# The first loads, semaphore counts and two small activations of a two-layer trunk kernel are put in another order

## The reference

```python
for i in range(2):                                   # DEPTH layers, x is (1, 512, 1024) f32
    h = rms_norm(x, attn_norm_w[i])
    proj = h @ w_in[i]                               # 1024 x 7456
    dq, dk, dv, cq, ckv, krope, xq, gates = split(proj)
    # differential attention (8 heads), rope on the first 16 of 64 columns
    y_a = (rms_norm(diff_attention(rope(dq), rope(dk), dv, lam)) * (1 - lam_init)) @ w_o_diff[i]
    # latent attention: q and kv from low-rank cq, ckv, rope on 32 columns
    y_b = causal_attention(q_full, k_full, v_m) @ w_o_mla[i]
    # cross-attention into 256 memory tokens
    mk, mv = split(rms_norm(mem, mem_norm_w[i]) @ w_mem_kv[i])
    y_c = softmax_attention(xq, mk, mv) @ w_o_cross[i]
    g_a, g_b, g_c = split(sigmoid(gates))
    x = x + (g_a * y_a + g_b * y_b + g_c * y_c) @ w_out[i]
    f_gate, f_up = split(rms_norm(x, ffn_norm_w[i]) @ w_gate_up[i])
    x = x + (silu(f_gate) * f_up) @ w_down[i]
return rms_norm(x, final_norm_w)
```

## Time and profile before

| | |
|---|---|
| median of 3 runs | 1964.63 us |
| the profiled execution's own time | 1964.07 us |
| its span, first to last instruction | 1961.9 us |
| TensorE busy | 1947.8 us, 99% |
| TensorE weight loads busy | 1632.6 us, 83% |
| VectorE busy | 1037.2 us, 53% |
| ScalarE busy | 935.8 us, 48% |
| GpSimd busy | 1074.4 us, 55% |
| mean granted TensorE clock | 0.999 |

### The profile page before, as it was taken

How to read it: one execution, slowest core, us unless ns; L and a number is a source line. 1 busy time by engine, 2 the same in 40 slices (tenths; PEclk the granted TensorE clock), 3 DMA queues, 4 the chain that set the end, 5 groups by cost and what they waited for, 6 DMA issues and landing times.

```text
span 1961.9 us, 28882 instructions
## 1 busy us (share of the span) xinstructions
PE 1947.8 (99%) x9340; PEld 1632.6 (83%) x9340; DVE 1037.2 (53%) x1900; ACT 935.8 (48%) x1665; POOL 1074.4 (55%) x1422
## 2 busy tenths in 40 slices
PE   8999999999999999999999999999999999999998
PEld 7888888888888888888888888888888888888887
DVE  6445888887655333321144658888876443333111
ACT  6444666776544322233344456776674342222332
POOL 6654454445554555557765645344445555555674
PEclk9999999999999999999999999999999999999999
DMA  6443233224543333333344323223356333333232
GB/s 195 128 148 92 76 91 87 81 76 140 183 145 96 102 95 98 94 115 89 109 138 120 111 85 92 81 76 89 90 158 191 113 99 94 98 96 96 84 92 91
DMA packets 356001, 212.61 MB, mean 108 GB/s; under 512 B 14274, under 2 KB 339906, under 8 KB 355396
## 3 DMA queue, kind: packets, MB, share of 16 engines
q1 hardware_dynamic: 338288, 173.32, 30.7%
q10 hardware_dynamic: 17620, 38.07, 5.5%
HBM read 190.88 MB, written 20.45 MB: 108 GB/s over the span
## 4 chain that ended last, share of the span: by engine, by line
PE 98%; POOL 1%; DVE 0%; issue 0%; DMA 0%; ACT 0%; SPq 0%; POOLq 0%
PE proj L602 24%; PE proj L604 24%; PE proj L603 24%; PE score L602 2%; PE score L603 2%; PE score L604 2%; PE flip L656 2%; PE score L638 2%; PE score L816 1%; PE score L818 1%; PE score L642 1%; PE score L641 1%; PE att L583 1%; PE att L584 1%; PE att L582 1%; PE score L830 1%
## 5 line engine op out<-in xcount | busy, mean ns | idle before, releaser
L564 POOL TENSOR_TENSOR w_lo<-raw,w_hi 128x256 fp32r<-128x256 f32 x1376 | 1069.3, 809 | 866.1 <-ACT w_hi L1109 864.9
L602 PE MATMUL proj<-h_hi,w_hi 128*128 128x512 f32 x1584 | 626.3, 395 | 0.6 <-DVE h_lo L1977 0.3
L604 PE MATMUL proj<-h_hi,w_lo 128*128 128x512 f32 x1584 | 618.1, 390 | 0.0
L603 PE MATMUL proj<-h_lo,w_hi 128*128 128x512 f32 x1584 | 616.9, 389 | 0.0
L1109 ACT ACTIVATE w_hi<-raw 128x1024 fp32r<-128x1024 f32 x344 | 362.5, 1055 | 195.4 <-PE proj L604 55.2
L604 PEld LDWEIGHTS proj<-h_hi,w_lo 128*128 128x128 f32 x1584 | 297.3, 188 | 63.3
L602 PEld LDWEIGHTS proj<-h_hi,w_hi 128*128 128x128 f32 x1584 | 297.6, 188 | 60.6 <-issue 0.9
L603 PEld LDWEIGHTS proj<-h_lo,w_hi 128*128 128x128 f32 x1584 | 297.7, 188 | 58.9 <-issue 0.2
L602 PE MATMUL proj<-hid_hi,w_hi 128*128 128x512 f32 x330 | 129.0, 391 | 0.0
L604 PE MATMUL proj<-hid_hi,w_lo 128*128 128x512 f32 x330 | 128.5, 389 | 0.0
L603 PE MATMUL proj<-hid_lo,w_hi 128*128 128x512 f32 x330 | 128.4, 389 | 0.0
(11 more groups left out here) (420 smaller groups left out, 3147.2 us busy)
## 6 DMA issues: line engine op xcount, KB each, us to landing
raw<-in_w_in SPq DMA_DIRECT2D x224, 256.0 KB, 3.1
raw<-in_w_gate_up SPq DMA_DIRECT2D x176, 256.0 KB, 3.0
raw<-in_w_down SPq DMA_DIRECT2D x96, 192.0 KB, 2.5
gate_in<-gate_scratch ACTq DMA_DIRECT2D x48, 256.0 KB, 4.1
gate_scratch<-gate_out ACTq DMA_DIRECT2D x46, 256.0 KB, 2.0
raw<-in_w_mem_kv SPq DMA_DIRECT2D x32, 256.0 KB, 2.9
raw<-in_w_o_diff SPq DMA_DIRECT2D x32, 256.0 KB, 2.9
raw<-in_w_out SPq DMA_DIRECT2D x32, 256.0 KB, 2.9
```

Of the source, the lines that this page charges most:

```text
L564: ins = g.tensor_tensor(w_lo[s][:, cols], raw[s % 2][:, cols], w_hi[s][:, cols].bitcast(F32), ALU.subtract)
L602: mm(o, hi[:, c:c + width], rh, start=start and k == 0, stop=False)
L603: mm(o, hi[:, c:c + width], rl, start=False, stop=False)
L604: ins = mm(o, lo[:, c:c + width], rh, start=False, stop=stop and k == n - 1)
```

## The change

SP: the first slot's two halves are now issued ahead of all of x; then come two quarters of x, the second slot's two halves, the other two quarters, and the memory tokens. ScalarE's `start_counts` goes from ScalarE's program into TensorE's, behind the warm-up matmuls and ahead of the first `flip_x`. ScalarE issues the load of the positions ahead of that of the gains. TensorE transposes four tiles of x ahead of its first weight unit where it did six, and then two ahead of tile 2 and two ahead of tile 4, where it did two ahead of tile 2. ScalarE makes the two sines behind the second tile, and the third slot's copy behind the memory tokens' exponential.

```diff
@@ sync
-            load_x(0)
@@
                 slot(l, "N", 0, 0, *whole(w_in, l, C_XQ))
                 if l == 0:
-                    for quarter in range(1, 4):
-                        load_x(quarter)
+                    load_x(0)
+                    load_x(1)
                 slot(l, "N", 0, 1, *gate(l, GATES_N))
                 if l == 0:
+                    load_x(2)
+                    load_x(3)
                     sp.dma_start(mem_in[:, :, :], ...).then_inc(in_mem, 16)
@@ tensor
             for i in range(WARM):
                 mm(proj[0][:, 0:P], ident[:, :], ident[:, :], start=i == 0, stop=i == WARM - 1)
+            start_counts(pe, "act")
@@
-            for k in range(KD - 2):
+            for k in range(KD // 2):
                 flip_x(k)
@@
                 def tile_split(k):
-                    if l == 0 and k == 2:
-                        flip_x(KD - 2)
-                        flip_x(KD - 1)
+                    if l == 0 and k in (2, 4):
+                        flip_x(k + 2)
+                        flip_x(k + 3)
@@ scalar
+            act.dma_start(pos_i[:, :], positions[:, :]).then_inc(in_pos, 16)
             act.dma_start(gains[:, 0:GAIN_COLS], gain_cols[:, :]).then_inc(in_gain, 16)
-            act.dma_start(pos_i[:, :], positions[:, :]).then_inc(in_pos, 16)
             act.wait_ge(const_ready, 1)
-            start_counts(act, "act")
@@
             for k in range(KD // 2):
                 first_tile(k)
+                if k == 1:
+                    act.wait_ge(pre_vec, 1)
+                    sc.activation(sin_t[:, :, :], ang[:, :, :], ACT.Sin)
+                    sc.activation(half_t[:, :, :], ang[:, :, :], ACT.Sin, scale=0.5).then_inc(pre_act, 1)
             first_slot(1)
@@
             copy(xT[:, 4, :], x_bank[4][:, :]).then_inc(x_gate, 1)
-            act.wait_ge(pre_vec, 1)
-            sc.activation(sin_t[:, :, :], ang[:, :, :], ACT.Sin)
-            sc.activation(half_t[:, :, :], ang[:, :, :], ACT.Sin, scale=0.5).then_inc(pre_act, 1)
...
-            first_slot(2)
...
             sc.activation(mem_rstd[:, :], mem_rstd[:, :], ACT.Exp, scale=-0.5).then_inc(pre_act, 1)
+            first_slot(2)
             act.wait_ge(x_gate, 1)
```

## The result

| kernel | median us | runs | range us | ratio to before |
|---|---|---|---|---|
| before | 1964.70 | 12 | 1963.72 to 1966.80 | |
| after | 1967.91 | 12 | 1965.90 to 1968.75 | 1.0016 [1.0008, 1.0023] |

The change costs 3.2 us (1967.91 - 1964.70). The profiled execution took 1967.82 us with a span of 1965.5, 3.6 us more than before's 1961.9. The number forecast was 1967.5. The sum behind it was +2.9 us, all at `x_sum`. The trace shows something else: 0.8 us there, 2.3 us at a wait which the prediction doesn't have, and 0.2 us in small pieces between the two. A right number came out of wrong steps.

What follows compares the result with a forecast made beforehand. TensorE, with 98% of the chain of waits, was taken as the bound, decided at `x_sum`. +1.9 us (squares of x) and +1.0 (clock) gave +2.9: profiled 1964.07 becomes 1967.0, median 1967.5; range 1963.0 to 1969.2.

Steps and rivals of the forecast that it cites:

- The sum: Whole kernel: +1.9 us at the squares of x plus +1.0 us for the clock, +2.9 us in all.
- its own test: Start and beyond: wrong if transposes start before 8 us, `x_sum` is passed before 31.4, or anything behind 40 us differs.
- What bounds the kernel: Whole kernel: TensorE carries 98% of the chain of waits; the bet is when it passes `x_sum`, 31.42 us before.
- That late split is free.: Third slot's `w_lo`: ready at 27.1 us or a little later, needed by TensorE at 27.8; no cost.
- behind `x_sum` all moves together; tightest place 0.7 us: After `x_sum`: everything shifts alike; tightest at the first scores, `qT` done at 38.8 for a matmul at 39.51.
- The counts behind the warm-up: TensorE's start: 37 counts take 5.7 us, from 4.7 to 10.4, so transposes start at 10.3 instead of 5.18.
- The loop-end row: TensorE around 860 us: loop's end at 859.7, preceding matmul started at 860.09, so the sequencer is only 0.4 us ahead.
- x lands at 6.7: Loads at the start: x's first quarter, now behind the first weights, lands at about 6.7 us.
- +1.9 at the squares of x: ScalarE's second square of x: starts at 26.1 us instead of 24.19, and `x_sum` follows in step.
- Rival B: TensorE's start: counts run beside the warm-up, end at 8.0, clock holds; -0.4 us, 1964.2; chance 0.11.
- The clock, +1.0: TensorE's start: idle from 5.3 to 10.3 drops it to 1.2 GHz until 13.5 to 15.5; costs +1.0 us.

Runs made afterwards that it cites:

- a_split_early: The kernel after with the third slot's copy back ahead of ScalarE's table load; 1964.57 us, ratio 1.0001.
- a_exps_first: The kernel after with ScalarE's cross-attention exponentials moved ahead of its eighth weight tile copy, the third split still late; 1964.25 us, ratio 0.9998.
- a_counts_act: The kernel after with the 37 counts back on ScalarE, ahead of its table load; 1964.59 us, ratio 1.0002.
- a_act_warm14: The kernel after with the counts back on ScalarE and 14 warm-up matmuls instead of 7; 1966.50 us, ratio 1.0008.
- b_loads_flips: The kernel before with only the change's order of loads (first weights ahead of x) and of transposes; 1964.59 us, ratio 1.0000.
- b_counts_exps: The kernel before with ScalarE's counts on TensorE and the cross-attention exponentials ahead of the eighth weight tile copy; 1964.43 us, ratio 1.0000.
- b_counts_pe: The kernel before with only ScalarE's 37 counts moved to TensorE behind the warm-up; 1964.05 us, ratio 0.9999.

## Why the prediction's number was right and its steps were not

By its own test it was wrong: transposes ahead of 8 us and a difference behind 40 us were to refute it, and both came.

- **What bounds the kernel.** "All that the change touches lies ahead of `x_sum`" was the wrong frame. The third split sits at the head of a ring of loads whose lateness travels. TensorE's own list of waits can't show that: a margin of 1.6 us is no wait.
- **"That late split is free."** This step failed, and with it "behind `x_sum` all moves together; tightest place 0.7 us". It followed the third tile to its own reader and no further. What is moved on GpSimd's path frees a raw buffer, and so sets when the fifth tile's load is issued. In the profile the wait is 2.3 us of the lateness, and taking it away brought the median back by all of the 3.2 us (a_split_early, a_exps_first). The late split is not its only source: it takes the counts on TensorE as well, since a_counts_act keeps the late split and has no wait.
- **The counts behind the warm-up.** Failed. Their size was right (37 in 5.5 us, 0.15 each), their start was 2.3 instead of 4.7. The loop-end row showed a lead of 0.4 us in the steady state, where the engine is always fed; it says nothing about a start at which the instructions are already there. By the Trainium skill ("TensorE: Matmul & The Clock Gate", opening table) TensorE queues 64 instructions, so the counts run beside the warm-up; the trace agrees for 28 instructions. With 56 the lead was about 33, which the page's number doesn't explain.
- **x lands at 6.7.** Mis-sized: its first quarter needed 5.7 us from its issue at 1.92 and landed at 7.6. This and the counts hold the transposes to the same 7.8, 2.5 us ahead of the forecast.
- **+1.9 at the squares of x.** Came out as +1.0 at 25.23, although the transposes were only 2.7 us late and not 5.1. (The forecast also calls 24.19 the start of the squares; the first of the four started at 21.56, and 24.19 is the second.) Rival B had priced a start at 8.0 at -0.4 with the clock holding. Its counts came true and its clock did not. Where the clock did hold, in a_act_warm14 with transposes from 7.89, the second square started at 23.58, 0.6 us earlier than before: near B's price, as far as one profile can tell.
- **The clock, +1.0.** The half rate came, up to 13.95 us, inside the range given. But it was to be a fall after an idle stretch, and no record shows full rate before it: the warm-up ended at 5.51 without having reached it. The price, where it could be tested, was 0.75 at `x_sum` (a_act_warm14 against a_counts_act), which is within the scatter of single profiles.
- **The sum.** +0.8 at `x_sum` for a forecast of +2.9, and +2.3 from a cost put at zero. The first is within the scatter, and no median shows it: b_loads_flips passed `x_sum` at 32.92 and a_split_early at 32.16, with medians like before's. That the numbers meet is luck.

Settled: the wait at line 838 makes the slowdown, and either the place of one copy or the time of one ring removes it. The place of the copy gains nothing by itself where no split is late (b_counts_exps 1964.43, b_counts_pe 1964.05). Open: why b_loads_flips shows 1.5 us in its profile and nothing in its median. (The 0.4 us in b_counts_pe's profile go with the one slow landing told above.) The order of the transposes and that of ScalarE's first two DMAs were not tried by themselves.

## What to carry to other kernels

Follow a moved instruction through the buffer that it frees, load by load, until something stops waiting for a DMA; its own reader is only the first stop. A ring's lateness costs nothing until an in-order engine meets it ahead of work that others wait for, so look for a copy that waits for a DMA in front of a short, urgent operation, and swap them. And write down margins beside waits: 1.6 us of margin was worth more here than all waits in the list.

## What the runs showed of the hardware

- A scaling by VectorE (TENSOR_SCALAR, 128x256 f32) took 0.34 to 0.36 us alone (a_exps_first) and 0.81 to 0.90 beside GpSimd's TENSOR_TENSOR (after), while GpSimd's stayed at 0.74 in the median. By the Trainium skill ("Advanced Engine Details and Errata", VectorE Performance Modes) VectorE's second port is shared with GpSimd, so that instructions of VectorE that use both ports and GpSimd's block each other. The trace agrees with a loss on VectorE's side: 4 instructions take 1.14 us beside next to none, 1.67 to 1.69 partly beside, 3.12 fully. It shows none on GpSimd's, and not which port was held.
- A semaphore count cost 0.15 us on TensorE's sequencer and 0.078 on ScalarE's; on TensorE's it ran beside 28 queued instructions, and 33 ahead at the most.
- The granted clock was not the same from one execution to the next for the same work: the kernel after and a_exps_first are the same program up to 40 us, and the first full-rate record was at 13.95 in the one and at 5.67 in the other (there it fell to half again from 9.08 to 12.50). The clock's column shows 1.00 in 8 to 13.9 us of after for lack of a record; the distance of the matmuls (0.43 against 0.23 us) is what tells the rate there.
